# A two-block transformer kernel on one core: x in column halves, small gathers and angles behind the first weight chunks

## The reference

```python
proj = x @ w_in                       # 256x1024 @ 1024x2120
q, k, v, iq, ik, iw = jnp.split(proj, A_SPLITS, axis=-1)
ang = positions.astype(jnp.float32)[..., None] * inv      # rotary_tables
cos, sin = jnp.cos(ang), jnp.sin(ang)
iq = partial_rotary(iq.reshape(bsz, L, IDX_HEADS, IDX_DIM), cos, sin)
ik = partial_rotary(ik, cos, sin)
s = jnp.einsum('bqhd,bsd->bqhs', iq_b, ik) * IDX_DIM ** -0.5
score = jnp.einsum('bqh,bqhs->bqs', iw_b, jax.nn.relu(s))
_, sel = lax.top_k(score, top_k)      # 64 keys for each query
```

## Time and profile before

| | |
|---|---|
| time, median of 3 runs | 1258.32 us (1257.95 to 1259.39) |
| span of the profiled execution | 1255.9 us |
| TensorE busy | 1234.8 us, 98% |
| VectorE busy | 855.9 us, 68% |
| ScalarE busy | 593.2 us, 47% |
| GpSimd busy | 93.0 us, 7% |
| moved by DMA | 221.06 MB, 176 GB/s on average |

### The profile page before, as it was taken

One profiled execution on the slowest core, in us unless ns is written; L12 is line 12 of the kernel. 1 busy time (PEld: TensorE's weight loads), 2 busy tenths in 40 slices (PEclk: granted clock), 3 DMA queues, 4 the chain that ended last, 5 costly groups with the idle time before them and its releaser, 6 DMA issues.

```text
span 1255.9 us, 19256 instructions
## 1 busy us (share of the span) xinstructions
PE 1234.8 (98%) x8277; PEld 1065.3 (85%) x8277; DVE 855.9 (68%) x919; ACT 593.2 (47%) x725; POOL 93.0 (7%) x226
## 2 busy tenths in 40 slices
PE   8989999999999999999999999999999999999998
PEld 7878888888888888888988888887997888888887
DVE  6787766666666676666776666668587667666675
ACT  5664543344743543344654444344562445434434
POOL 4341000001000200000201000001000100000000
PEclk9999999999999999999999999999999999999999
DMA  8424665555633765554625655555654247555642
GB/s 278 156 81 135 203 200 188 183 199 149 207 135 125 244 201 179 190 201 138 224 75 184 192 194 199 178 194 201 197 164 160 103 142 236 199 179 192 201 145 90
DMA packets 131268, 221.06 MB, mean 176 GB/s; under 512 B 6984, under 2 KB 99424, under 8 KB 131184
## 3 DMA queue, kind: packets, MB, share of 16 engines
q1 hardware_dynamic: 128160, 209.83, 50.2%
q0 software_dynamic: 3024, 10.01, 2.7%
HBM read 218.77 MB, written 1.05 MB: 175 GB/s over the span
## 4 chain that ended last, share of the span: by engine, by line
PE 81%; DVE 8%; ACT 5%; DMA 2%; issue 2%; POOL 1%; SPq 0%; ACTq 0%; DVEq 0%; POOLq 0%
PE ps L757 18%; PE ps L607 18%; PE ps L759 9%; PE ps L584 8%; PE ps L585 8%; PE ps L586 8%; PE ps L718 4%; DVE wlo L1780 4%; ACT whi L1322 2%; PE ps L771 2%; ACT rot L1347 1%; DMA raw<-in_mlp_w_up 1%; DMA raw<-in_ffn_w_in 1%; DVE buf L1859 1%; PE ps L928 1%
## 5 line engine op out<-in xcount | busy, mean ns | idle before, releaser
L1780 DVE TENSOR_TENSOR wlo<-raw,whi 128x2048 fp32r<-128x2048 f32 (+3 forms) x203 | 452.3, 2241 | 175.9 <-ACT whi L1322 174.1
L1322 ACT ACTIVATE whi<-raw 128x2048 fp32r<-128x2048 f32 (+3 forms) x203 | 376.8, 1868 | 73.6 <-DMA raw<-in_hgrn_w_in 23.6
L757 PE MATMUL ps<-xhl,whi 128*128 128x512 f32 x1088 | 271.4, 391 | 0.0
L757 PEld LDWEIGHTS ps<-xhl,whi 128*128 128x128 f32 x1088 | 198.3, 189 | 37.2
L607 PE MATMUL ps<-whi,xhl 128*128 128x512 f32 (+1 forms) x864 | 212.8, 379 | 4.0 <-DVE wlo L1780 1.6
L607 PEld LDWEIGHTS ps<-whi,xhl 128*128 128x128 f32 x864 | 152.0, 188 | 34.9 <-issue 2.6
L584 PE MATMUL ps<-whi,hh 128*128 128x512 f32 x432 | 169.0, 391 | 0.0
L585 PE MATMUL ps<-whi,hl 128*128 128x512 f32 x432 | 168.6, 390 | 0.0
L586 PE MATMUL ps<-wlo,hh 128*128 128x512 f32 x432 | 168.1, 389 | 0.0
L759 PEld LDWEIGHTS ps<-xhl,wlo 128*128 128x128 f32 x1088 | 148.4, 190 | 10.6
L759 PE MATMUL ps<-xhl,wlo 128*128 128x256 f32 x1088 | 151.7, 282 | 0.0
(11 more groups left out here) (331 smaller groups left out, 1303.0 us busy)
## 6 DMA issues: line engine op xcount, KB each, us to landing
raw<-in_ffn_w_in SPq DMA_DIRECT2D x44, 1024.0 KB, 5.1
raw<-in_mlp_w_up SPq DMA_DIRECT2D x32, 1024.0 KB, 5.4
raw<-in_mlp_w_down SPq DMA_DIRECT2D x32, 1024.0 KB, 4.9
raw<-in_ffn_w_down SPq DMA_DIRECT2D x22, 1024.0 KB, 4.9
raw<-in_hgrn_w_in SPq DMA_DIRECT2D x16, 1024.0 KB, 5.4
raw<-in_b_w_in SPq DMA_DIRECT2D x12, 1024.0 KB, 5.3
raw<-in_ple_w_gate SPq DMA_DIRECT2D x8, 1024.0 KB, 6.3
raw<-in_a_w_in SPq DMA_DIRECT2D x6, 1024.0 KB, 5.3
```

Source lines behind the costliest of these rows:

```text
L757: mm(bank(b + f), w[0][:, kk, P * f : P * f + P], xhl[:, kk, :, :].rearrange("p a n -> p (a n)"), start=(kk == 0), stop=False)
L1322: a.activation(whi[:, slot, 0:w], raw[:, slot, 0:w], ACT.Copy).then_inc(s["hi_done"], 1)
L1780: v.tensor_tensor(wlo[:, slot, 0:w], raw[:, slot, 0:w], whi[:, slot, 0:w].bitcast(F32), ALU.subtract).then_inc(s["lo_done"], 1)
```

## The change

x is loaded in column halves: 512 features of both tiles of tokens ahead of chunk 0, the other 512 of both between chunks 1 and 2. TensorE, ScalarE and VectorE take x in that order too: the transposes of the second half stand behind the products of chunk 0 (chunks 0 and 1 need the first half only). The dummies become 12, 4 and 8. The products of the index queries go in the order hi x hi, lo (of x) x hi, hi x lo, and the wait for a chunk's lo part stands ahead of the third group only. GpSimd issues its six gathers only when chunk 2 has landed, and clears `kT` before. The angles are computed behind the split of chunk 3, the second set behind that of the small chunk, and the cosines around that of the k chunk. The short vectors are transposed behind the last chunk of the index queries.

```diff
--- before.py
+++ after.py
@@ -228,12 +228,15 @@
 
         @block.sync
         def _(sp):
-            def load_x(tt):
-                sp.dma_start(x[:, tt, :], t["x"][0, tt * P : (tt + 1) * P, :]).then_inc(s[f"x_landed{tt}"], 16)
+            def load_x(hf):
+
+                cs = slice(512 * hf, 512 * hf + 512)
+                for tt in range(TT):
+                    sp.dma_start(x[:, tt, cs], t["x"][0, tt * P : (tt + 1) * P, cs]).then_inc(s[f"x_landed{tt}{hf}"], 16)
 
             load_x(0)
             for n in range(N_CHUNKS):
-                if n == 1:
+                if n == 2:
                     load_x(1)
                 src, k, cols = source[n]
                 if n >= RING:
@@ -383,13 +386,6 @@
             g.affine_select(out=ident[:, :], in_=ident[:, :], compare_op=ALU.not_equal, fill=1.0, base=0,
                             pattern=[[-1, P]], channel_multiplier=1).then_inc(s["ident_done"], 1)
 
-            for w, name in enumerate(("positions", "positions_2")):
-                pool.dma_start(posi[:, w, :], t[name][0].rearrange("(t p) -> p t", p=P), allow_slow_non_contiguous=True).then_inc(s["pos_landed"], 16)
-            pool.dma_start(vrow[V_BA : V_BA + 4, :], t["b_b_a"][0].rearrange("(r p) -> r p", p=P)).then_inc(s["vrow_landed"], 16)
-            pool.dma_start(vrow[V_QN : V_QN + 2, :], t["mla_q_norm_2"][0].rearrange("(r p) -> r p", p=P)).then_inc(s["vrow_landed"], 16)
-            pool.dma_start(vrow[V_KVN : V_KVN + 2, :], t["mla_kv_norm_2"][0].rearrange("(r p) -> r p", p=P)).then_inc(s["vrow_landed"], 16)
-            pool.dma_start(vrow[V_LB : V_LB + 16, :], t["hgrn_lb_logits_2"].rearrange("l (h p) -> (l h) p", p=P)).then_inc(s["vrow_landed"], 16)
-
             def load_ln(i):
 
                 layer = (i // 2) % 2
@@ -427,6 +423,14 @@
             for c, f in enumerate(freq_a + freq_m):
                 last = g.memset(inv[:, c : c + 1], f)
             last.then_inc(s["inv_done"], 1)
+            step(g.memset(kT[:, :, :, :], 0.0))
+            pool.wait_ge(s["raw_landed2"], 16)
+            for w, name in enumerate(("positions", "positions_2")):
+                pool.dma_start(posi[:, w, :], t[name][0].rearrange("(t p) -> p t", p=P), allow_slow_non_contiguous=True).then_inc(s["pos_landed"], 16)
+            pool.dma_start(vrow[V_BA : V_BA + 4, :], t["b_b_a"][0].rearrange("(r p) -> r p", p=P)).then_inc(s["vrow_landed"], 16)
+            pool.dma_start(vrow[V_QN : V_QN + 2, :], t["mla_q_norm_2"][0].rearrange("(r p) -> r p", p=P)).then_inc(s["vrow_landed"], 16)
+            pool.dma_start(vrow[V_KVN : V_KVN + 2, :], t["mla_kv_norm_2"][0].rearrange("(r p) -> r p", p=P)).then_inc(s["vrow_landed"], 16)
+            pool.dma_start(vrow[V_LB : V_LB + 16, :], t["hgrn_lb_logits_2"].rearrange("l (h p) -> (l h) p", p=P)).then_inc(s["vrow_landed"], 16)
 
             def note(ins):
 
@@ -452,8 +456,6 @@
 
                     pool.wait_ge(s[signal], tt + 1)
 
-
-            step(g.memset(kT[:, :, :, :], 0.0))
             pool.wait_ge(s["tables_done"], 1)
             def rotate_both(v, n_heads):
 
@@ -761,12 +763,8 @@
 
             def turn_tile(j, src, tt):
 
-                if j == 0:
-                    pe.wait_ge(s[f"x_landed{tt}"], 16)
-                    pe.wait_ge(s["ident_done"], 1)
                 for hf in range(2):
-                    if j > 0:
-                        pe.wait_ge(s["src_ready"], ready(j, tt, hf, j in BY_HALF))
+                    pe.wait_ge(s["src_ready"], ready(j, tt, hf, j in BY_HALF))
                     for q in range(4):
                         last = nc.tensor.transpose(ps[:, 4 + 2 * tt + hf, P * q : P * q + P],
                                                    src[:, tt, P * (4 * hf + q) : P * (4 * hf + q) + P], ident[:, :])
@@ -966,20 +964,43 @@
                 for q in range(n):
                     nc.tensor.transpose(ps[:, 1, P * (q % 4) : P * (q % 4) + P], ident[:, :], ident[:, :])
 
+            def turn_input(tt, hf):
+
+                pe.wait_ge(s[f"x_landed{tt}{hf}"], 16)
+                for q in range(4):
+                    last = nc.tensor.transpose(ps[:, 4 + 2 * tt + hf, P * q : P * q + P],
+                                               x[:, tt, P * (4 * hf + q) : P * (4 * hf + q) + P], ident[:, :])
+                last.then_inc(s["turned"], 1)
+
+            def index_queries(q):
+
+                n = first["dsa_iq"] + q
+                w = weights(n, 2, 512)
+                hf = q // 2
+                pe.wait_ge(s["hi_done"], n + 1)
+                for step, (part, w_part) in enumerate(((0, 0), (1, 0), (0, 1))):
+                    if step == 2:
+                        take(n)
+                    for tt in range(TT):
+                        if q % 2 == 0 and step < 2:
+                            pe.wait_ge(s["turn_lo" if part else "turn_hi"], TT * hf + tt + 1)
+                        for kk in range(2):
+                            last = mm(bank(2 + tt), (xh, xl)[part][:, 2 * q + kk, P * tt : P * tt + P], w[w_part][:, kk, :],
+                                      start=(q == 0 and step == 0 and kk == 0), stop=(q == 3 and step == 2 and kk == 1))
+                last.then_inc(s["w_done"], 1)
+
             keep_fed(12)
-            turn_tile(T_X0, x, 0)
-            keep_fed(16)
-            turn_tile(T_X0, x, 1)
-            take(first["dsa_iq"])
+            turn_input(0, 0)
+            keep_fed(4)
+            turn_input(1, 0)
+            keep_fed(8)
+            index_queries(0)
             for tt in range(TT):
-                pe.wait_ge(s["turn_lo"], 2 * tt + 2)
-                last = rows(first["dsa_iq"], 2, 512, 0, KD, [(tt, slice(0, 512), bank(2 + tt))])
-            last.then_inc(s["w_done"], 1)
+                turn_input(tt, 1)
             for q in range(1, 4):
-                by_rows(first["dsa_iq"] + q, 2, 512, 2 * q, KD, [(tt, slice(0, 512), bank(2 + tt)) for tt in range(TT)])
-                if q == 1:
-                    pe.wait_ge(s["vrow_landed"], 64)
-                    nc.tensor.transpose(ps[:, 6, 0:V_ROWS], vrow[:, :], ident[0:V_ROWS, 0:V_ROWS]).then_inc(s["vrow_turned"], 1)
+                index_queries(q)
+            pe.wait_ge(s["vrow_landed"], 64)
+            nc.tensor.transpose(ps[:, 6, 0:V_ROWS], vrow[:, :], ident[0:V_ROWS, 0:V_ROWS]).then_inc(s["vrow_turned"], 1)
             n = first["dsa_small"]
             take(n)
             w = weights(n, KD, A_SMALL)
@@ -1527,16 +1548,23 @@
                         act.wait_ge(s["w_done"], n0 + 5)
                     a.activation(y[:, u // 2, 512 * (u % 2) : 512 * (u % 2) + 512], bank(u), ACT.Sigmoid).then_inc(s["sig_done"], 1)
 
-            turned_tile(T_X0, 0)
-            until(first["dsa_iq"])
-            turned_tile(T_X0, 1)
+            def input_hi(tt, hf):
+
+                act.wait_ge(s["turned"], TT * hf + tt + 1)
+                a.activation(xh[:, 4 * hf : 4 * hf + 4, P * tt : P * tt + P],
+                             bank(4 + 2 * tt + hf).rearrange("p (k n) -> p k n", k=4), ACT.Copy).then_inc(s["turn_hi"], 1)
+
+            for tt in range(TT):
+                input_hi(tt, 0)
             until(first["dsa_iq"] + 1)
+            for tt in range(TT):
+                input_hi(tt, 1)
+            until(first["dsa_small"])
             for w, (sn, cs) in enumerate(((sinA, cosA), (sinM, cosM))):
                 act.wait_ge(s["angle_done"], w + 1)
                 a.activation(sn[:, :, :], cs[:, :, :], ACT.Sin)
                 a.activation(cs[:, :, :], cs[:, :, :], ACT.Sin, scale=0.5).then_inc(s["sines_done"], 1)
-                until(first["dsa_iq"] + 3)
-            until(first["dsa_k"])
+                until(first["dsa_k"])
             act.wait_ge(s["w_done"], first["dsa_iq"] + 4)
             a.activation(kvi[:, 0, 512:1024], bank(2), ACT.Copy).then_inc(s["iq_act"], 1)
             until(first["dsa_q"])
@@ -2069,10 +2097,19 @@
                     step(v.tensor_tensor(y[:, tt, c0:c1], y[:, tt, c0:c1], side[:, tt, c0:c1], ALU.mult))
                     v.tensor_tensor(x[:, tt, c0:c1], x[:, tt, c0:c1], y[:, tt, c0:c1], ALU.add).then_inc(s["src_ready" if layer == 0 else "out_ready"], 1)
 
-            turned(T_X0, 0)
-            until(first["dsa_iq"])
-            turned(T_X0, 1)
+            def input_lo(tt, hf):
+
+                dve.wait_ge(s["turn_hi"], TT * hf + tt + 1)
+                hi = xh[:, 4 * hf : 4 * hf + 4, P * tt : P * tt + P]
+                lo = xl[:, 4 * hf : 4 * hf + 4, P * tt : P * tt + P]
+                v.tensor_tensor(lo, bank(4 + 2 * tt + hf).rearrange("p (k n) -> p k n", k=4), hi.bitcast(F32), ALU.subtract).then_inc(s["turn_lo"], 1)
+
+            for tt in range(TT):
+                input_lo(tt, 0)
             until(first["dsa_iq"] + 1)
+            for tt in range(TT):
+                input_lo(tt, 1)
+            until(first["dsa_iq"] + 3)
 
             dve.wait_ge(s["pos_landed"], 32)
             dve.wait_ge(s["inv_done"], 1)
@@ -2086,14 +2123,13 @@
```

(5 more changed lines are left out.)

## The result

The changed kernel is slower: **1261.25 us** median (1260.35 to 1262.08) against 1258.34 us (1256.79 to 1259.39) for the kernel before, 11 runs of each. The ratio is 1.0025, its 95% interval 1.0017 to 1.0033. The forecast was 1255.7 with a range of 1254.3 to 1257.9. The profiled spans are 1259.5 and 1255.9 us, 3.6 apart, where the medians differ by 2.9.

A forecast was written before the change was run, and what follows sets the result against it. TensorE, busy 98% of the span, was taken as the bound, with only first-stage idle time to gain. Profiled span 1255.9 minus 2.6 gives 1253.3; plus 2.4 from span to median, 1255.7 us, range 1254.3 to 1257.9.

The forecast's parts named there:

- The start: Up to the first product: half loads of x cause no delay, products begin at 8.08 against 9.03 us.
- The stage: Index queries' products: TensorE sets the time from 8.08 us; small projection at 20.2 instead of 22.82, 2.6 us gained.
- What transfers must do: Loads of x and chunks 0 to 2, ahead of the gathers, done at about 9.3 us at 393 GB/s.
- The gathers, moved: GpSimd's six gathers, issued behind chunk 2: positions land at 14.5 us, vectors at 17, at no cost.
- rival of late vectors: Vectors' transposition: TensorE waits for late vectors; slower by 0.2% with latency over 12.3 us; chance 0.04.
- VectorE behind the splits: VectorE from 15.9 us: k's lo part ends at 22.7, TensorE asks at 23.1, 0.4 us to spare.
- Gathers land late, VectorE is late: Rival: late positions push angles and k's lo part; gain 1.0 to 2.0, time 1256.3 to 1257.3 us; chance 0.25.
- Behind the stage: Later work shifts with TensorE; GpSimd's rotations run 23.9 to 33.1 us, wanted at 34.5, so covered.
- Rotations collide: Rival: another slow GpSimd rotation beside VectorE ends the rotations at 35.2, 0.7 behind; gain 1.9, 1256.4 us; chance 0.10.
- TensorE stays slow at the start: Rival: first sixteen products run at half pace after fewer dummies and 1.1 us idle; 1259.2 us; chance 0.04.

The follow-up runs named there:

- xwhole: Changed kernel with x loaded as two whole tiles of tokens, both ahead of chunk 0; 1259.41 us, one run.
- dvewait: Changed kernel with VectorE waiting for GpSimd's rotated index operands before it splits the second query chunk; 1256.82 us, ratio 0.9996.
- xone: Changed kernel with each column half of x loaded by one DMA instead of two; 1259.77 us, one run.
- fill: Changed kernel with 20 dummy transposes ahead of TensorE's wait for the rotated index operands; 1262.75 us, ratio 1.0041.
- order: Kernel before with only the order of the index queries' products and their wait for the lo part changed; 1259.59 us, ratio 1.0016.
- gearlynw: Changed kernel with only the six gathers put back at the start, no wait on VectorE; 1261.39 us, ratio 1.0022.
- anglesback: Changed kernel with gathers at the start and angles, sines and cosines in their old places; 1262.19 us, ratio 1.0032.
- gearly: Changed kernel with gathers back at the start and VectorE's second query split held until the rotations end; 1257.53 us, ratio 0.9995.
- orderwait: Kernel before with the new order of the index queries' products and VectorE's second query split held until the rotations end; 1256.62 us, ratio 0.9988.
- beforewait: Kernel before with only VectorE's second query split held until the rotations end; 1258.01 us, ratio 1.0000.

## Why the prediction was wrong

*The start* failed. "I take no delay" for the half loads: chunk 0 landed at 7.93, 2.45 us later than before, so the first product began at 9.06 and not at 8.08, 0.98 us lost. The row for the reason was there in part: nothing in the trace showed two loads of 256 KB in a row, and I priced them by the rate of large ones. The slow stretch from 3 to 5 us comes with the four half loads in all seven traces that have them; how much of the late landing it makes is not shown, as chunk 0 was late in xwhole without it (7.60).

*The stage* was right: 11.58 us forecast from first to last product, 11.65 measured (9.06 to 20.71), no gap in it.

*What transfers must do* failed in its size: chunk 2 landed at 12.40, not at 9.3. From 2 us on I had the engines run at 393 GB/s throughout; the 2.6 MB then give 8.7 us, so the sum itself was 0.6 too high and the miss is 3.7.

*The gathers, moved* failed with it. From their issue (13.04) the vectors' 5.5 us to landing were inside the bounds, but the issue was 3.7 us late, and the last vector took 5.5 us with only two large loads queued, where I had taken 4.5; the last landed at 21.76 instead of 17, and the transposition waited. For the vectors I had taken 0.55 us; they took 1.26, 0.71 more. With the 0.98 and 0.07 of the stage this makes up the 1.77 us between the forecast 20.2 and the measured 21.97. (The busy row's "nine queued loads" are seven: two of x and five chunks.) The rival of late vectors had named this wait, but let it cost nothing up to a latency of 7.2 us, as it counted from an issue at 12.5.

*VectorE behind the splits* was right by luck: k's lo part ended at 24.81 against a request at 24.87, 2.1 and 1.8 us later than forecast, so that 0.06 of the 0.4 us to spare were left. In dvewait, xone and fill, with the same order of work, TensorE did wait for it (0.50, 0.89 and 0.27 us): the rival *Gathers land late, VectorE is late* is what these show.

*Behind the stage* is the step that turned the sign. "Rotations 23.9 to 33.1, wanted at 34.5. Covered." I shifted the chain as a block of 9.2 us and looked at its margin to TensorE alone. It began at 25.95, 2.05 us later than forecast, and ended at 39.05, 5.95 later, while TensorE asked at 36.1. The length was no constant: it holds 5.0 us of work and 2.0 us for each subtraction that it meets, and before it met two of them (I had read one). Its margin to the next, the pair at 34.22, was 0.13 us, not the 2.95 to TensorE's request. The rival *Rotations collide* had the mechanism, with one more hold, an end 0.7 behind TensorE and a chance of 0.10; in truth it was two more holds, 3.0 us of idle time, and the clock's 1.6 behind it. All five kernels with an earlier TensorE and no wait (after, fill, xone, xwhole, order) had exactly four holds and a chain of 13.1 us. So had gearlynw, where TensorE was 1.0 us later than before: there VectorE was the late one, as it does the second cosines between k's lo part and its copy. In these six VectorE's first subtraction follows its copies at once and the next starts 5.3 us behind the chain's start; in before and anglesback the first waits for ScalarE (0.85 and 1.01 us), the next starts 6.3 and 6.8 us behind, and there are two holds.

*TensorE stays slow at the start*, chance 0.04, did not happen in the changed kernel, though it idled for 1.82 us there, nor in anglesback behind 3.12 us; it did in gearlynw, behind 2.26 us.

The sum of the parts: small projection -0.85, idle time +2.8, clock +1.6, hence +3.5 in the trace. Had only the start and the gathers been mis-sized, the time would be near that of dvewait: 1256.82, or 1257.8 by its ratio to before, inside the range.

## What to carry to other kernels

Where a chain on GpSimd runs beside VectorE's long instructions with two SBUF inputs, its length depends on when they start: list the starts of both engines side by side, and take as margin the distance from the chain's end to the next such start, not that to whoever waits for the result. An edit that makes TensorE earlier also makes the following splits earlier, so test it together with a wait that keeps the one split that nobody needs yet behind the chain; here a single such line was worth 3 to 4 us (after and dvewait, gearlynw and gearly, order and orderwait), and nothing where the chain was covered (beforewait). To a gap of TensorE of 2 to 3 us, as they are here, add some 1.5 us for the low clock that may follow it.
